# A two-layer hybrid backbone in fp32: the first weight block of four weight stages moved into the stage ahead of each, and two reordered VectorE queues

## The reference

```python
def mixing_sublayer(h_lat, h_ctx, w_in, ...):
    p_lat = jnp.split(h_lat @ w_in, split_at, axis=-1)
    ...                       # hgrn2_mix | gqa_mix | na_mix
    y_lat = jnp.concatenate([hg_l, gq_l, na_l], axis=-1) @ w_out
def swiglu(h, w1, w2):
    gate, up = jnp.split(h @ w1, 2, axis=-1)
    return (jax.nn.silu(gate) * up) @ w2
# per layer
x = layer_norm(DN_ALPHA * x + m[2] * mixing_sublayer(modulate(x, m[0], m[1])), ln_g[l, 0], ln_b[l, 0])
x = layer_norm(DN_ALPHA * x + m[5] * swiglu(modulate(x, m[3], m[4])), ln_g[l, 1], ln_b[l, 1])
```

## Time and profile before

| | us |
|---|---|
| three runs | 4243.36, 4246.05, 4252.34 (median 4246.05) |
| profiled execution | 4241.93 |
| its span | 4240.5 (1.4 lie around it) |
| PE busy | 3715.3 (88%) |
| DVE busy | 1757.7 (41%) |
| ACT busy | 1067.3 (25%) |
| mean granted TensorE clock | 0.934 of full speed |
| DMA | 318.72 MB, mean 75 GB/s |

### The profile page before, as it was taken

How to read it: one execution, slowest core, us unless ns; L and a number is a source line. 1 busy time by engine, 2 the same in 40 slices (tenths; PEclk the granted TensorE clock), 3 DMA queues, 4 the chain that set the end, 5 groups by cost and what they waited for, 6 DMA issues and landing times. The chain is left out here.

```text
span 4240.5 us, 52173 instructions
## 1 busy us (share of the span) xinstructions
PE 3715.3 (88%) x22306; PEld 3001.3 (71%) x22306; DVE 1757.7 (41%) x1933; ACT 1067.3 (25%) x1473; POOL 208.5 (5%) x118
## 2 busy tenths in 40 slices
PE   5999467979897999999997799567978969999997
PEld 3888345458775888888886688445468758888886
DVE  3112667555424232323225212667655343333334
ACT  2000332446314111111113200322556141111113
POOL 0000003003000000000000000003012000000000
PEclk7999779989898999999998899779989989999998
DMA  7433532031422111111113522431041311211111
GB/s 237 97 86 102 200 110 59 7 102 47 148 64 66 43 32 30 45 45 30 30 35 99 142 88 83 166 113 46 11 115 56 106 40 45 59 45 45 55 37 42
DMA packets 294823, 318.72 MB, mean 75 GB/s; under 512 B 42398, under 2 KB 261130, under 8 KB 294410
## 3 DMA queue, kind: packets, MB, share of 16 engines
q1 hardware_dynamic: 269034, 267.43, 21.1%
q0 software_dynamic: 6912, 30.15, 2.3%
q10 hardware_dynamic: 18720, 18.88, 1.4%
HBM read 247.78 MB, written 71.59 MB: 75 GB/s over the span
## 5 line engine op out<-in xcount | busy, mean ns | idle before, releaser
L511 PE MATMUL psum<-h_hi,f_whi 128*128 128x512 f32 (+1 forms) x1760 | 481.8, 371 | 43.0 <-DVE f_wlo L1134 43.0
L511 PE MATMUL psum<-h_hi,f_wlo 128*128 128x512 f32 (+1 forms) x1760 | 480.9, 371 | 0.0
L511 PE MATMUL psum<-h_lo,f_whi 128*128 128x512 f32 (+1 forms) x1760 | 480.8, 371 | 0.0
L511 PE MATMUL psum<-h_hi,w_hi 128*128 128x512 f32 (+1 forms) x1392 | 368.6, 368 | 86.5 <-DVE w_lo L656 54.5
L511 PEld LDWEIGHTS psum<-h_hi,f_whi 128*128 128x128 f32 x1760 | 308.5, 188 | 102.3 <-DVE f_wlo L1134 43.5
L1140 DVE SCALAR_TENSOR_TENSOR y<-psum,mods,y 128x1024 f32<-128x1024 f32 (+1 forms) x264 | 260.4, 1014 | 257.9 <-PE psum L511 257.0
L511 PE MATMUL psum<-h_lo,w_hi 128*128 128x512 f32 (+1 forms) x1392 | 366.6, 366 | 0.0
L511 PE MATMUL psum<-h_hi,w_lo 128*128 128x512 f32 (+1 forms) x1392 | 366.0, 366 | 0.0
L511 PEld LDWEIGHTS psum<-h_lo,f_whi 128*128 128x128 f32 x1760 | 308.3, 188 | 58.9
L511 PEld LDWEIGHTS psum<-h_hi,f_wlo 128*128 128x128 f32 x1760 | 308.1, 188 | 58.8
L511 PEld LDWEIGHTS psum<-h_hi,w_hi 128*128 128x128 f32 x1392 | 239.3, 190 | 133.5 <-issue 29.0
(11 more groups left out here) (268 smaller groups left out, 5278.1 us busy)
## 6 DMA issues: line engine op xcount, KB each, us to landing
f_raw<-in_w_ffn_in SPq DMA_DIRECT2D x88, 512.0 KB, 6.1
ada_w<-in_w_ada SPq DMA_DIRECT2D x30, 1024.0 KB, 10.9
w_raw<-in_w_in SPq DMA_DIRECT2D x48, 512.0 KB, 5.3
proj_cm<-lin_stage POOLq DMA_DIRECT2D x38, 640.0 KB, 4.2
f_raw<-in_w_ffn_out SPq DMA_DIRECT2D x44, 512.0 KB, 3.8
ada_w<-in_w_ada ACTq DMA_DIRECT2D x18, 1024.0 KB, 5.7
na_qk<-proj_cm SPq DMA_DIRECT2D x48, 320.0 KB, 8.0
hg_pj<-proj_cm SPq DMA_DIRECT2D x20, 640.0 KB, 9.3
```

Of the source, the lines that this page charges most:

```text
L511: ins = nc.tensor.matmul(out[:, t0:t0 + tn], w, h[:, t0:t0 + tn], start=start and n == 0, stop=stop and n == 2)
```

## The change

`Lead` is a pair of buffers for one weight block and its neighbour (`lead_raw`, `lead_hi`, `lead_lo`), allocated across two stages, with four steps that are placed into the stage ahead of `linear` or `swiglu`: `load` (SP, two transfers of 512 KB: units 0 and 1, or gate 0 and up 0), `upper` (ACT's cast of the first), `lower` (DVE's subtraction) and `products` (PE, into set A). The stage after it starts with unit 1, or with up 0.

- In `front`: `load` behind the input loads, ahead of the stores of `x_cm`; `upper` ahead of the first `h_hi`; `lower` behind `modulated(0)` and `modulated(2)`; PE multiplies input block j as soon as `h_lo[j]` is written.
- In `residual_norm` (before `swiglu` in both layers, and before `linear` of layer 1): `load` first; `upper` behind the first square; `lower` behind the second `centre`; the products run in pieces of tokens. Mean and variance move to banks 3, 4 and 5, 7.
- In `hgrn`, `out(lvl - 1)` stands behind the new keys and queries, ahead of the other halves.
- In `na_attention`, `result(n - 1)` is done behind `negmax(n + 2)`.

```diff
+class Lead:
+    def load(self, sp):
+        for n in range(2):
+            sp.dma_start(self.raw[:, n].rearrange("p (j q) -> p j q", j=KB), self.src[n]).then_inc(self.s_w[n].h, 16)
+    def upper(self, act):
+        act.wait_ge(self.s_w[0].h, self.s_w[0].at(16))
+        self.k.nc.scalar.copy(self.hi[:], self.raw[:, 0]).then_inc(self.s_hi.h, 1)
+    def lower(self, dve):
+        dve.wait_ge(self.s_hi.h, self.s_hi.at(1))
+        self.k.nc.vector.tensor_tensor(self.lo[:], self.raw[:, 0], self.hi[:].bitcast(F32), ALU.subtract).then_inc(self.s_lo.h, 1)
+    def products(self, pe, j, piece, start, stop):
+        cols = slice(j * P, (j + 1) * P)
+        return three_products(self.k.nc, self.k.set_a, piece, self.hi[:, cols], self.lo[:, cols], self.h_hi[:, j], self.h_lo[:, j], start, stop)
...
 # front, tensor engine
                 mod.turn(pe, n_m - 1)
+                pe.wait_ge(lead.s_lo.h, lead.s_lo.at(1))
+                pe.wait_ge(s_x.h, s_x.at(TT))
+                for j in range(KB):
+                    pe.wait_ge(s_lo.h, s_lo.at(j + 1))
+                    ins = lead.products(pe, j, token_chunks(NT), j == 0, j == KB - 1)
+                ins.then_inc(lead.s_mm.h, 1)
...
 # residual_norm
+        pieces = [(0, 2 * T)] + ([(2 * T, 2 * T), (4 * T, T)] if n_c % 2 else [(2 * T, T), (3 * T, T)])
+                def lead_piece(n):
+                    t0, tn = pieces[n]
+                    if n == 0:
+                        pe.wait_ge(lead.s_lo.h, lead.s_lo.at(1))
+                    pe.wait_ge(s_lo.h, s_lo.at((t0 + tn) // T))
+                    for j in range(KB):
+                        ins = lead.products(pe, j, [(t0, tn)], j == 0, j == KB - 1)
...
+                    if lead and i == n_c - 2:
+                        lead_piece(0)
                 mod.turn(pe)
+                for n in range(1, len(pieces) if lead else 0):
+                    lead_piece(n)
...
 # linear, sync engine: load(0, 0, 0) and load(1, 1, 0) removed; unit, hi and lo start at 1
-                load(0, 0, 0)
-                load(1, 1, 0)
...
 # swiglu: gate block 0 is neither loaded, split nor multiplied here
-                    up(0, p * 2)
                     if not first:
+                        up(0, p * 2)
...
 # na_attention, vector engine
-                    result(n)
+                    if n:
+                        result(n - 1)
+                result(N - 1)
...
 # hgrn, vector engine: behind the new keys and queries
+                    if lvl:
+                        out(lvl - 1)
                     after(dve, s_ck, lvl + 1)
                     scored(dve, 1)
...
-                    if lvl:
-                        out(lvl - 1)
```

More of the change, by code:

```diff
@@ L65, in token_chunks, with in_pairs @@
     return [c for c in CHUNKS if c[0] < tokens]
-def in_pairs(e, n, body):
+def in_pairs(e, n, body, first=0):
+    for u in range(first, 2 if first else 0):
+        body(u, u, 0)
     if n // 2 > 1:
-        with e.Fori(0, n // 2) as i:
+        with e.Fori(1 if first else 0, n // 2) as i:
             for s in range(2):
@@ L364, in _ @@
                     load(t)
+                lead.load(sp)
                 for t in range(0, TT, 2):
@@ L450, in _ @@
                 modulated(2)
+                lead.lower(dve)
                 for j in range(KB):
@@ L585, in done, with linear @@
         self.s_st.done(6 * 16)
-def linear(k, l, src, units, tokens, h_hi, h_lo, widths=None):
+def linear(k, l, src, units, tokens, h_hi, h_lo, lead, widths=None):
     nc = k.nc
@@ L819, in mix_out, with residual_norm @@
         x.done(KB)
-def residual_norm(k, l, sub, tokens, y, h_hi, h_lo, last, mod_ranges):
+def residual_norm(k, l, sub, tokens, y, h_hi, h_lo, last, mod_ranges, lead=None):
     nc = k.nc
@@ L1028, in _ @@
                         centre(i + 1)
+                    if i == 0 and lead:
+                        lead.lower(dve)
                     if i < n_c:
@@ L1052, in residual_norm, with swiglu @@
         s_out.done(16 * n_c)
-def swiglu(k, l, tokens, h_hi, h_lo, y):
+def swiglu(k, l, tokens, h_hi, h_lo, y, lead):
     nc = k.nc
@@ L1085, in loads @@
                 def loads(j, first=False):
-                    for n in range(3):
+                    for n in range(2 if first else 0, 3):
                         if not first:
@@ L2544, in hgrn, with project_in @@
     s_yd.done(16 * len(groups))
-def project_in(k, l, h_hi, h_lo):
+def project_in(k, l, h_hi, h_lo, lead):
     w_in = k.a["w_in"][l].rearrange("(j p) n -> p j n", p=P)
@@ L2551, in project_in @@
         context[u] = SEQ
-    linear(k, l, lambda u: w_in[:, :, bass.ds(u * P, P)], IN_W // P, NT, h_hi, h_lo, widths=context if l == DEPTH - 1 else None)
+    linear(k, l, lambda u: w_in[:, :, bass.ds(u * P, P)], IN_W // P, NT, h_hi, h_lo, lead, widths=context if l == DEPTH - 1 else None)
 def mix(k, l, ctx, mods):
@@ L2579, in build @@
             h_lo = k.sb(st, "h_lo", [P, KB, NT], F32R)
-            front(k, h_hi, h_lo, [(0, 0, 2)])
-            project_in(k, 0, h_hi, h_lo)
+            lead = Lead(k, st)
+            front(k, h_hi, h_lo, [(0, 0, 2)], lead.of_linear(0, h_hi, h_lo))
+            project_in(k, 0, h_hi, h_lo, lead)
         for l in range(DEPTH):
```

97 lines of the change are left out of this document (63 added, 34 removed).

## The result

| | before | after |
|---|---|---|
| median of the runs | 4245.72 us (4243.36 to 4252.34, 4 runs) | 4151.37 us (4146.43 to 4154.62, 4 runs) |
| profiled execution | 4241.93 us | 4146.43 us |
| PE busy | 3715.3 us (88%) | 3721.5 us (90%) |

What follows compares the result with a forecast made beforehand. PE, busy 88%, was taken as the bound: its work plus its standstills. Lead blocks 60.8, recurrence 20.5 and 5.5, neighbourhood attention 2.8 sum to 89.6 us, giving 4152.3 profiled and 4156 as median; range 4134 to 4180.

Steps and rivals of the forecast that it cites:

- new-start rule: Four lead blocks: the second block starts at the last lead product's end plus 0.28 and 2.36 us, plus the old clock loss.
- the last 256-token piece: First norm, layer 0: the last lead products end at 1325.7 us, or 1327.6 at the lower clock.
- Rival (d): Linear of layer 1: the 16.7 us gained come back as a wait before unit 4, total 4173 us; chance 0.05.
- 0 was the right end and not 2.7: Front: delay of the modulation rows by the two new loads, taken as 0, with 2.7 us as the other end.
- I take 20.5 us: Recurrence, layer 0: gain from the earlier merge, out of 21.4 us of DVE idle, with short PE pauses allowed for.
- The ring on DVE: Recurrence, layer 0: each level is a closed ring of 14.84 us for 9.0 us of work; the earlier merge ends DVE's idle.
- rival (a): Recurrence: a ring remains, on PE and the modulation pieces; the gain of 26 us becomes 12, total 4170 us; chance 0.11.
- Moved back, the maximum comes about 0.5 us earlier, 2.5 us in five: Neighbourhood attention: gain at layer 0's five changes of head, plus 0.3 us for layer 1.
- the bound of 17 us: Neighbourhood attention, layer 0: the most to gain, if all five stalls vanished with the lower clock that follows, 5 x (1.76 + 1.7).
- rival (c): Attention stalls vanish with their lower clock (4142 us), or second blocks start at full clock (4148); both 4134; chance 0.11.
- Rival (e): Neighbourhood attention: PE's next product waits for the later result in each of 108 tiles; slower, 4267 us at 1.0 each; chance 0.02.
- (b): Lead products run at 1.2 GHz throughout: 9.6 us lost in front, 1.9 in norms, 14 with the DMA's 2.7, 4170; chance 0.09.

Runs made afterwards that it cites:

- leads_only: The changed kernel with the old VectorE order put back in the recurrence and in neighbourhood attention, leaving the four lead blocks alone: 4178.48 us, 0.9845 of the kernel before.
- hgrn_small: The changed kernel, but in both recurrences modulation pieces behind the third load only one of their eight input blocks, all products still made: 4139.56 us.

## Why the prediction was right, and where only its sum was

**The lead blocks held step by step.** The new-start rule (end of the last product, 0.28, 2.36) gives 75.7 + 0.28 + 2.36 = 78.3 for 78.57 and 1275.5 + 2.64 = 1278.1 for 1278.16. The stage ahead of linear of layer 1 ends with its store, at the same place of the trace as before, and its products are hidden. What was off: the last 256-token piece in layer 0 took 4.6 us instead of 3.2, since PE had been idle for 2.15 us and fell to the lower clock in it (up 0 came 7.3 us behind the last h_lo instead of 5.8), and in layer 1 up 0 lost 3.0 us to the lower clock instead of 1.6. Rival (d), the gain of linear coming back before unit 4, is 0.39 us.

**The modulation rows were not late, as far as can be told.** First h_lo in the four traces without the two loads: 58.5, 60.4, 56.0, 58.6 us; in eight with them 53.6 to 59.8, mean 57.3, although a subtraction stands ahead. So 0 was the right end and not 2.7; the spread of some 6 us between executions hides anything smaller. From the first h_lo to the first transposes of the recurrence it was 388.7 to 389.2 us and is 369.1 to 370.6 now: 19 us, of which the first h_lo's own delay of up to 1 us goes off, about 18.

**The recurrence of layer 0 failed in one step**: "I take 20.5 us", with two or three pauses of 0.6 us for PE. The ring on DVE is gone (period 9.30 us, 459.98 to 469.28, for 9.1), but PE got pauses that the old waits had covered. With most of the traffic taken away the stretch is 73.3 us, 21.8 under the mean of four traces in the old order (95.1), near the 20.5; no run has the old order with little traffic, so how much of the 21.8 is the order's alone stays open. With the full traffic the gain is 16.0 on the mean of four traces. That is between the forecast and rival (a), by another mechanism than (a) named: not PE's work, its instructions.

**Neighbourhood attention failed too**: "Moved back, the maximum comes about 0.5 us earlier, 2.5 us in five". The stall did shorten, by 0.7 us (3.7 in five) where 0.5 had been worked out. What was taken for the bound of 17 us, the lower clock going with it, is what happened, and what rival (c) said for this place. The argument against (c) looked at whether a stall remains, not at whether its new length is one that the clock had been seen to follow. In that stage of the trace before no stall of PE lay between 0.86 and 1.76 us, so 2.8 was a choice at one end of a wide gap.

**Rival (e) had no ground**: PE's product with the values waits for no result (its only waits there are for ACT's copies, 2.3 us in all of layer 0). (b) was wrong: lead products in the front are at full clock from 63 us on. The forecast of 89.6 against 95.5 is therefore better than its parts, and by luck: +12.7 in the attention against -3.8 in the recurrence and -4.0 between the stages, with 1.5 of earlier rows on top. The term that was mis-sized most is the attention's, 2.8 us for a measured 15.5.

## What to carry to other kernels

When a stall is shortened and not removed, work out two prices, its own length and the clock behind it, and take the clock's as a case of its own with a real chance; here it was some three quarters of the edit's gain (15.5 - 3.7 of 15.5). When waits on a slow partner are taken away, ask what else they had covered: with many small matmuls and a busy DMA, here it was the arrival of the engine's own instructions. And once a block's products are moved ahead of a stage change, the cast and the subtraction of the next block are the new gap; move them too where there is space.

## What the hardware showed that was not expected

- PE pauses at steps of 127 matmuls (each with its weight load) when nothing else holds it, and goes on 1.2 to 1.6 us behind the end of a 16 KB instruction packet, 60 times of 60. Beside full DMA traffic the longest pause was 5.32 us, at the same place 3.65 with half of the pieces' data and 0.43 with an eighth; with next to no traffic pauses of 1.05 and 1.65 us remain.
- Five stalls of 1.45 us at the changes of head left the clock at 1.00. With stalls of 1.70 us, two of the heads read 0.88 over 28 us and took some 3 us longer than the others (31.7 and 31.9 for 28.7).
- PE can be busy nearly throughout and stay at the lower level: 14.42 of 15.00 us at 0.50 in the preparation of queries and keys.
- The same idle does not always have the same effect: in the front PE stood 2.86 us ahead of unit 1 in seven traces. The block behind it took 14.2 us in five of them, and 15.7 in the other two (leads_only, hgrn_small), where the first two microseconds read 0.80 and 0.79 and not 1.00. What decides that stays open.
- The arrival of the front's modulation rows varies by some 6 us between executions of nearly the same code, which is as much as one of the smaller parts of this change.
